# Projections and recurrent branch of a hybrid layer: gate weights and banks shared across the borders between them, rows of a branch split in place and loaded at once

## The reference, cut to what matters

```python
xn = _rmsnorm(x, norm1_g)
z = xn @ w_in                      # (1088 rows, 1024) @ (1024, 7184)
u_x, u_g, q, k, v, f_logit, g_rnn, g_attn = split(z)
conv_out = causal_conv(u_x, width 4) + conv_b
h_seq, h_last = _rg_lru(conv_out, ...)        # block-diagonal gates, scan over time
rnn_y = (gelu(u_g) * h_seq) @ w_rnn_out
attn_y = attention(q, k, v, ...) @ w_attn_out
x = x + (sigmoid(g_rnn) * rnn_y + sigmoid(g_attn) * attn_y) @ w_o
x = x + _hier_moe(_rmsnorm(x, norm2_g), ...)  # 32 experts, top 2
```

## Time and profile before

| what | us |
|---|---|
| median of 3 timed runs (lowest, highest) | 2629.52 (2626.59, 2631.68) |
| profiled execution, its own time | 2625.33 |
| its span, first to last instruction | 2623.1 |
| TensorE busy in the span | 2200.3 (84%) |
| VectorE, ScalarE busy | 1345.8 (51%), 1138.6 (43%) |
| first matmul of `project` 0, of `recurrent`, of `project` 1 | 1078.40, 1282.64, 1558.84 |
| first matmul of the stage behind `project` 1 | 1767.97 |

### The profile page before, as it was taken

One profiled execution on the slowest core, in us unless ns is written; L12 is line 12 of the kernel. 1 busy time (PEld: TensorE's weight loads), 2 busy tenths in 40 slices (PEclk: granted clock), 3 DMA queues, 4 the chain that ended last, 5 costly groups with the idle time before them and its releaser, 6 DMA issues. The chain is left out here.

```text
span 2623.1 us, 37125 instructions
## 1 busy us (share of the span) xinstructions
PE 2200.3 (84%) x11260; PEld 1774.6 (68%) x11260; DVE 1345.8 (51%) x1570; ACT 1138.6 (43%) x1545; POOL 226.8 (9%) x297
## 2 busy tenths in 40 slices
PE   4469898888989887799899959987937999999991
PEld 2356676666767664699888849985825777777770
DVE  5433545546354554411255542223256888888884
ACT  3223444534344343211156632112205777777770
POOL 0210202202020110000000000000001010110102
PEclk9779999999999997899999979998958999999995
DMA  3310202113020110311122232113126999999986
GB/s 88 67 33 10 83 24 59 47 36 83 8 75 26 41 50 10 111 46 48 50 84 86 83 101 65 45 59 126 41 105 251 374 399 394 394 399 394 394 328 237
DMA packets 199069, 351.22 MB, mean 134 GB/s; under 512 B 19852, under 2 KB 127544, under 8 KB 198920
## 3 DMA queue, kind: packets, MB, share of 16 engines
q1 hardware_dynamic: 181544, 293.55, 31.8%
q0 software_dynamic: 13872, 44.35, 5.5%
q10 hardware_dynamic: 3584, 12.58, 1.2%
HBM read 301.87 MB, written 48.58 MB: 134 GB/s over the span
## 5 line engine op out<-in xcount | busy, mean ns | idle before, releaser
L2208 DVE TENSOR_TENSOR e_w_lo<-e_raw,e_w_hi 128x2048 fp32r<-128x2048 f32 x192 | 434.4, 2290 | 91.0 <-ACT e_w_hi L2135 72.8
L2135 ACT CAST e_w_hi<-e_raw 128x2048 fp32r<-128x2048 f32 x192 | 365.9, 1908 | 61.9 <-PE e_y_ps L103 36.1
L101 PE MATMUL proj_ps<-w_qkv_hi,xh 128*128 128x384 f32 x544 | 232.0, 427 | 24.9 <-PEq L286 19.1
L102 PE MATMUL proj_ps<-w_qkv_lo,xh 128*128 128x384 f32 x544 | 186.4, 343 | 0.0
L103 PE MATMUL proj_ps<-w_qkv_hi,xl 128*128 128x384 f32 x544 | 186.3, 342 | 0.0
L1155 PE MATMUL out_ps<-mT 128*128 128x512 f32 (+3 forms) x384 | 171.5, 529 | 3.6 <-DVEq L84 2.9
L101 PEld LDWEIGHTS proj_ps<-w_qkv_hi,xh 128*128 128x128 f32 x544 | 106.0, 195 | 52.3 <-issue 45.6
L1354 ACT ACTIVATE mT<-st_ps 128x512 f32<-128x512 f32 x192 | 93.8, 488 | 100.5 <-PE st_ps L1140 46.0
L1496 DVE TENSOR_REDUCE neg_part<-max_ps 128x1 f32<-128x512 f32 (+3 forms) x128 | 75.4, 589 | 88.9 <-PE max_ps L1081 42.8
L102 PEld LDWEIGHTS proj_ps<-w_qkv_lo,xh 128*128 128x128 f32 x544 | 105.4, 194 | 20.6 <-issue 15.6
L1078 PE MATMUL max_ps<-qk_high 66*128 66x512 f32 (+1 forms) x192 | 78.4, 408 | 45.8 <-DVE extra L1496 28.5
(11 more groups left out here) (420 smaller groups left out, 5407.5 us busy)
## 6 DMA issues: line engine op xcount, KB each, us to landing
e_raw<-w_gate_e SPq DMA_DIRECT2D x64, 1024.0 KB, 8.0
e_raw<-w_up_e SPq DMA_DIRECT2D x64, 1024.0 KB, 8.6
e_raw<-w_down_e SPq DMA_DIRECT2D x64, 1024.0 KB, 8.6
w_raw<-w_in SPq DMA_DIRECT2D x24, 512.0 KB, 4.6
slot_y<-e_y ACTq DMA_DIRECT2D x32, 384.0 KB, 6.1
slot_y<-zrows POOLq DMA_DIRECT2D x24, 352.0 KB, 4.2
mT<-cache_k SPq DMA_DIRECT2D x8, 1024.0 KB, 5.6
mT<-cache_v POOLq DMA_DIRECT2D x8, 1024.0 KB, 6.8
```

Source lines behind the costliest of these rows:

```text
L101: nc.tensor.matmul(out, a_hi, b_hi, start=start, stop=False)
L102: nc.tensor.matmul(out, a_hi, b_lo, start=False, stop=False)
L2135: sc.copy(w_hi[u][:, :], w.raw[c][:, :]).then_inc(wh_ready, 1)
L2208: v.tensor_tensor(w_lo[u][:, :], w.raw[c][:, :], w_hi[u][:, :], ALU.subtract).then_inc(wl_ready, 1)
```

## The change: what it does

- The raw weight tile, its high and low parts and the three banks `ux_ps` are allocated once, outside the three stages. `project` uses them for its gate, `recurrent` for its x weights.
- At the end of `project` 0, SyncE loads the first x weights of `recurrent` behind the last projection weights; ScalarE rounds them behind its last sigmoid and VectorE subtracts them ahead of its last multiplication. `recurrent` no longer does that for its first tile.
- At the end of `recurrent`, SyncE loads the first gate weights of `project` 1; ScalarE rounds them in its last step between the copies and the sigmoids, VectorE subtracts them behind the convolution, and TensorE does the gate product of `project` 1 behind its last small gate matmuls. `project` 1 begins with its projection product. The turning of the tails goes to `ug_ps`.
- The rows of a branch are loaded where their low part will stand (`b_parts[1]`, read as F32), and the subtraction writes over them. There is a place for each, so no load waits for an earlier row. In `project` 0 two rows are loaded ahead of the first projection weights and six behind them; in `project` 1 the projection weights come first, then all eight rows. Rows 2 and 3, 4 and 5, 6 and 7 share a semaphore each, and the waiter waits for both of a pair.

```diff
@@ recurrent
-        w_x, w_g = sb("r_wx", [P, KT, P]), sb("r_wg", [P, KT, P])
+        w_x, w_g = g.raw_x, sb("r_wg", [P, KT, P])
+        wx_split, wg_split = g.split_x, [sb(f"r_wg_{part}", [P, KT, P], F32R) for part in ("hi", "lo")]
-        ux_ps = ctx.enter_context(nc.psum_tensor("ux_ps", [P, N_THIRDS, BANK], F32))
+        ux_ps = g.ux_ps
 SP:
-                load_x(0)
                 load_g(0)
...
+                sp.wait_ge(x_split, KT)
+                sp.dma_start(w_x[:, :, :], g.w_in_k[:, :, COL_GATE_RNN:COL_GATE_RNN + P]).then_inc(g.gate_loaded, 16)
                 sp.wait_ge(tails_kept, 1)
 TensorE, behind the loop:
+                pe.wait_ge(g.gate_split, KT + 1)
+                pe.wait_ge(conv_ready, KT + 1)
+                one_product(ux_ps, wx_split).then_inc(g.gate_ready, 1)
                 pe.wait_ge(tails_ready, 1)
-                nc.tensor.transpose(ux_ps[...
+                nc.tensor.transpose(ug_ps[...
 ScalarE, step:
                     if more:
                         round_x(c + 1)
+                    else:
+                        act.wait_ge(g.gate_loaded, KT * 16 + 16)
+                        nc.scalar.copy(wx_split[0][:, :, :], w_x[:, :, :]).then_inc(g.gate_rounded, 1)
-                round_x(0)
 VectorE, step:
                     if more:
                         rest_x(c + 1)
+                    else:
+                        dve.wait_ge(g.gate_rounded, KT + 1)
+                        v.tensor_tensor(wx_split[1][:, :, :], w_x[:, :, :], wx_split[0][:, :, :], ALU.subtract).then_inc(g.gate_split, 1)
-                rest_x(0)
@@ project
-        w_raw = sb("_w", [P, KT, P])
+        w_raw, wg_split = g.raw_x, g.split_x
-        b_raw = [sb("_b0", [P, T_WIDE]), sig]
-        gate_ps = ctx.enter_context(nc.psum_tensor(tag + "_gate_ps", [P, N_THIRDS, BANK], F32))
+        b_raw = b_parts[1][:, :, :].bitcast(F32)
+        gate_ps = g.ux_ps
+        LOADS = (slice(0, 1), slice(1, 2), slice(2, 4), slice(4, 6), slice(6, 8))
 SP:
-                load_g(0)
+                if call == 0:
+                    load_g(0)
                 for k in range(KT):
-                    if k == 2:
+                    if k == 2 * (1 - call):
                         sp.wait_ge(g_split, before + 1)
                         load_p(0)
-                    if k >= 2:
-                        sp.wait_ge(b_split, before + k - 1)
-                    sp.dma_start(b_raw[k % 2][:, :], branch[k]).then_inc(b_loaded[k % 2], 16)
+                    sp.dma_start(b_raw[:, k, :], branch[k]).then_inc(b_loaded[load_of(k)], 16)
...
+                if call == 0:
+                    sp.wait_ge(p_split, KT)
+                    sp.dma_start(w_raw[:, :, :], g.w_in_k[:, :, COL_X:COL_X + P]).then_inc(g.x_loaded, 16)
 TensorE:
-                with pe.Fori(0, KT) as c:
...
+                if call == 0:
+                    gate(0)
+                proj(0)
+                with pe.Fori(0, KT - 1) as c:
+                    gate(c + 1)
+                    proj(c + 1)
 ScalarE, step:
+                    elif call == 0:
+                        act.wait_ge(g.x_loaded, 16)
+                        nc.scalar.copy(wg_split[0][:, :, :], w_raw[:, :, :]).then_inc(g.x_rounded, 1)
 VectorE, step:
+                    elif call == 0:
+                        dve.wait_ge(g.x_rounded, 1)
+                        v.tensor_tensor(wg_split[1][:, :, :], w_raw[:, :, :], wg_split[0][:, :, :], ALU.subtract).then_inc(g.x_split, 1)
```

More of the change, by code:

```diff
@@ L508, in _ @@
                         last.then_inc(gate_ready, 1)
+                pe.wait_ge(g.gate_split, KT + 1)
+                pe.wait_ge(conv_ready, KT + 1)
+                one_product(ux_ps, wx_split).then_inc(g.gate_ready, 1)
                 pe.wait_ge(tails_ready, 1)
-                nc.tensor.transpose(ux_ps[0:(2 * H + 2) * KT, 0, 0:P], tails[:, :, :].rearrange("p j c -> p (j c)"),
+                nc.tensor.transpose(ug_ps[0:(2 * H + 2) * KT, 0, 0:P], tails[:, :, :].rearrange("p j c -> p (j c)"),
                                     g.ident[:, :]).then_inc(tails_turned, 1)
@@ L629, in _ @@
                 dve.wait_ge(tails_turned, 1)
-                edge(v.tensor_copy(tails_T[0:(2 * H + 2) * KT, :], ux_ps[0:(2 * H + 2) * KT, 0, 0:P]), tails_kept)
+                edge(v.tensor_copy(tails_T[0:(2 * H + 2) * KT, :], ug_ps[0:(2 * H + 2) * KT, 0, 0:P]), tails_kept)
 def project(nc, g, sems, call, branch, w_out, gate_col, add, tag):
@@ L638, in project @@
         sb = lambda name, shape, dt=F32: ctx.enter_context(nc.sbuf_tensor(tag + name, shape, dt))
-        w_raw = sb("_w", [P, KT, P])
-        wg_split, wp_split = ([sb(f"_{n}_{part}", [P, KT, P], F32R) for part in ("hi", "lo")] for n in ("wg", "wp"))
+        w_raw, wg_split = g.raw_x, g.split_x
+        wp_split = [sb(f"_wp_{part}", [P, KT, P], F32R) for part in ("hi", "lo")]
         b_parts = [sb(f"_b_{part}", [P, KT, T_WIDE], F32R) for part in ("hi", "lo")]
         sig = sb("_sig", [P, T_WIDE])
-        b_raw = [sb("_b0", [P, T_WIDE]), sig]
-        gate_ps = ctx.enter_context(nc.psum_tensor(tag + "_gate_ps", [P, N_THIRDS, BANK], F32))
+        b_raw = b_parts[1][:, :, :].bitcast(F32)
+        gate_ps = g.ux_ps
         proj_ps = ctx.enter_context(nc.psum_tensor(tag + "_proj_ps", [P, N_THIRDS, BANK], F32))
@@ L648, in project @@
         before = call * KT
+        LOADS = (slice(0, 1), slice(1, 2), slice(2, 4), slice(4, 6), slice(6, 8))
+        load_of = lambda k: next(n for n, ks in enumerate(LOADS) if k < ks.stop)
+        b_count = lambda n: (16 * PAIRS if n >= 2 else 0) + 16 * (LOADS[n].stop - LOADS[n].start) * (call + 1)
         V_BEFORE = call * KT
@@ L689, in _, with gate @@
                     pe.sem_inc(proj_taken, 1)
-                with pe.Fori(0, KT) as c:
+                def gate(c):
                     pe.wait_ge(g_split, before + c + 1)
@@ L2369, in layer @@
         sem = lambda name: g.sem("p_" + name)
-        sems = (sem("g_loaded"), sem("p_loaded"), [sem(f"b_loaded{u}") for u in range(2)], sem("g_rounded"), sem("p_rounded"),
+        sems = (sem("g_loaded"), sem("p_loaded"), [sem(f"b_loaded{u}") for u in range(2)] + g.w_loaded, sem("g_rounded"), sem("p_rounded"),
                 sem("b_rounded"), sem("g_split"), sem("p_split"), sem("b_split"), sem("gate_ready"), sem("proj_ready"),
                 sem("sig_ready"), sem("proj_taken"), sem("chain_v"))
+        g.raw_x = front.enter_context(nc.sbuf_tensor("r_wx", [P, KT, P], F32))
+        g.split_x = [front.enter_context(nc.sbuf_tensor(f"r_wx_{part}", [P, KT, P], F32R)) for part in ("hi", "lo")]
+        banks = front.enter_context(ExitStack())
+        g.ux_ps = banks.enter_context(nc.psum_tensor("ux_ps", [P, N_THIRDS, BANK], F32))
+        g.x_loaded, g.x_rounded, g.x_split = g.sem("rx_loaded"), g.sem("rx_rounded"), g.sem("rx_split")
+        g.gate_loaded, g.gate_rounded, g.gate_split, g.gate_ready = sems[0], sems[3], sems[6], sems[9]
         project(nc, g, sems, 0, g.attn_T, g.w_attn_out, COL_GATE_ATTN, False, "pa")
@@ L2375, in layer @@
         project(nc, g, sems, 1, g.y_T, g.w_rnn_out, COL_GATE_RNN, True, "pr")
+        banks.close()
     with g.right:
```

22 lines of the change are left out of this document (12 added, 10 removed).

## The result

| kernel | timed runs, median (lowest to highest) | ratio to before, 95% interval |
|---|---|---|
| before | 2629.52 (2626.59 to 2631.68), 3 runs | |
| changed | 2603.62 (2601.66 to 2605.52), 3 runs | 0.9906 (0.9892 to 0.9919) |
| changed, timed again with five runs | 2605.35 (2602.35 to 2610.89), before 2630.09 | 0.9909 (0.9897 to 0.9922) |

The change is worth 25.9 us by the first medians and 24.7 by the second; 2604 was forecast. The profiled execution of the changed kernel took 2605.52 us, with a span of 2603.9.

What follows compares the result with a forecast made beforehand. TensorE's own rate bounds the projections, and late low parts of weight tiles cause its pauses at the borders. Gains of 2.2 + 8.1 + 15.3 = 25.6 us from the median 2629.5 give 2604, range 2599 to 2614.

Steps and rivals of the forecast that it cites:

- Border one: Attention to `project` 0: rows loaded at once let gate 1 start without a pause, 2.2 us gained.
- Border two: `project` 0 to `recurrent`: x weights prepared before the barrier, the clock stays up through a 2.2 us pause, 8.1 us gained.
- TensorE's start behind the barrier: At border two: TensorE starts at 1276.6, after SyncE's issue at 1276.33, between no delay and 1 us.
- End of `recurrent`: The added load, cast, subtraction and gate product fit into waits and cost nothing; 3.4 us left before the tails.
- Border three: `recurrent` to `project` 1: gate 0 gone from behind the barrier, gate 1 pauses 1.0 us, 15.3 us gained.
- The rows: At border three: rows land 1.33 us apart, and the last is split at about 1570.9.
- The clock: At border three: a pause of 1.0 us before gate 1 keeps the clock up, product 12.1 us; 2.8 us of the gain.
- rows over 2 us apart: Sign of being wrong: in `project` 1 rows land over 2 us apart, where 1.33 was forecast.
- The fallen clock: Rival: the clock falls in a shortened pause at border two or three, 2.8 us each: 2607 or 2609.5; chance 0.20.
- The flood: Rival: loads at once share the engines, weights land only with the last row: 2614; chance 0.07, with rows half as fast.
- Rows one by one: Rival: row loads don't overlap, each lands one full load time after the last; at 4.9 us a row 2645; chance 0.03.
- The moved product: Rival: the gate product moved into `recurrent` runs at the low clock, 21.8 us, tails 6.2 us late: 2610; chance 0.05.

Runs made afterwards that it cites:

- e3: The changed kernel with the rows loaded two at a time as before, weights and gate product still carried across the borders: 2619.35 us.
- e7: The changed kernel with the wait for the tail stores moved from `recurrent` to the end of `project` 1: 2608.78 us.
- e9: e7 with the last row of `y_T` stored by SyncE, not by GpSimd: 2601.00 us.
- e11: The changed kernel unaltered, timed once more beside e9 and e10 on the same chip: 2606.45 us.
- e5: The changed kernel, but in `project` 1 SyncE holds rows 2 to 7 back until row 0 is rounded: 2609.91 us.
- e10: e8 with the last row of `y_T` stored by SyncE: 2592.27 us.
- e8: The changed kernel with `project` 1's first sigmoid early, tail stores awaited late, its first projection weights loaded and split in `recurrent`: 2602.71 us.

## Why the prediction was right, and which terms were off

*Border one.* Right in mechanism and size: 2.0 for 2.2. The difference is a cold first product of 14.04 us where it had been 13.87; the pause is gone. Gate 1's weights were split at 1099.3, against the 1098.6 worked out, 5 us ahead of need.

*Border two.* Right in mechanism; the term of TensorE's start behind the barrier was too small. SyncE issued at 1274.28, TensorE began at 1275.13: 0.85 us, where 0.27 was taken within bounds of 0 and 1. That is the missing 0.6. The clock stayed through the pause of 2.58 us (product 12.06), and in every other trace with the carried x weights the product took 12.06 to 12.10. That it would stay was right, but the reason given for it, a pause nearer to 1.93 than to 2.88 us, does not hold: in e3 a pause of 1.92 us, at the very place of the 1.93, brought the clock down. So this part of the 8.1 us was in part luck.

*End of `recurrent`.* All its work was free, as forecast: the stretch from `ug_ps` to the tails is 248.11 us in both.

*Border three.* 12.8 for 15.3, and the other traces 14.0 and 13.3. Two terms were off. The rows: row 1 came 2.48 us behind row 0, not 1.33, and the last pair 15.9 us behind the first load, not 14.85. The back-to-back rows of before showed how two rows land, and I carried their distance to eight. Gate 1 so started 24.2 us behind the first load, not 23.25 (1575.6 - 1552.35): 1.0 us. The chain of 4.7 us from eighth row to gate 1 was exact (1562.23 to 1566.92). The clock: with the pause at 2.05 us and not 1.0, the product took 13.63 and not 12.1: 1.5 us. Together the missing 2.5. In the two other traces the pause was 1.1 to 1.2 us, the clock stayed, and the term is off by the rows alone.

*The signs of being wrong.* Of those named, "rows over 2 us apart" came between rows 0 and 1 in two of the three traces (2.48 and 2.15), though the time was near the forecast.

*The rivals.* The fallen clock came at border three, in one of three traces, for 1.5 us and not 2.8; e7 and e9, whose `project` 1 waits by the same chain, had it too. It was given 0.20, and 0.62 went to the forecast. The flood didn't come in the form given (weights landed 3.85 us behind their issue, as ever); a weaker form, rows at up to 1 us more, did at times. Rows one by one did not happen: 1.36 us a row in the stream. The moved product ran at 12.1.

The median of 2603.62 lies nearer to the 2604 than the terms deserve. Those sum to 25.6 and the traces show 22.4 to 23.8; the spread of the other stages made up the difference in the first timing and took it back in e11.

*What stays open.* Why a few of the sixteen shares of a row land up to 2 us after the others in one run and not in another; e5 shows that it happens without six more rows queued behind. What decides whether the clock falls in a pause of 1.9 to 2.6 us. And what of e10's median beyond its stages is more than spread.

## What to carry to other kernels

At a barrier between stages, ask for each engine what it needs first and whether it can be loaded and split in the shadow of the last product of the stage before. Where two such changes meet at one border, the two measured singly need not sum to the whole (here 11.1 us for 12.8 to 14.0). And before moving a wait, look at which engine comes last to the barrier: here the stores that SyncE waited for lay in the shadow of a drain on another engine.

## What the runs showed of the hardware

- A store issued by GpSimd shortly before a stage's end was followed, after it had landed, by a DRAIN of 2.67 us on GpSimd's queue, and the barrier waited for it. With the store issued from SyncE, GpSimd's own drain (2.59 us) started 17 us ahead of the turning of the tails, and the border was 4.1 us shorter (7.25 to 3.11), 0.9 of it because the store landed sooner.
- Of the 16 steps in which a load counts its semaphore up, a few can be up to 2 us behind the rest: in e11 fifteen of row 0's had come by 5.65 us behind the stage's first load and the last at 7.45, in e8 fifteen of row 1's by 5.73 and the last at 7.30.
- Of the pauses in front of gate 1 in `project` 1, those of 1.12, 1.22, 1.23 and 1.67 us left the clock up (the product behind the pause 12.1), those of 2.05, 2.15 (twice) and 2.36 us brought it down (13.63), and so did 2.88 in the kernel before (14.88). In front of gate 1 of `project` 0, 1.93 us left it up (12.1) and 1.92 us, in e3, brought it down (13.65). At border two pauses of 2.55 to 2.58 us left it up in all eleven traces that have them, product 12.06 to 12.10. The length of a pause alone doesn't tell. TensorE had been at the full clock through the whole last projection before border two, while ahead of the other pauses it had started cold one or two products earlier (first matmul 0.64 to 0.67 us); that this is the cause is not shown.
- With its operands ready, TensorE's first matmul behind border two came 0.82 to 0.86 us after SyncE's first load in all eleven traces. In the first of them six control instructions of TensorE (lines 493 to 496, 1274.37 to 1275.08) fill most of that, so it is what stands ahead of the loop as much as the barrier.
